# Experts' weights loaded in pairs of units: 32 KB contiguous per partition, two transfers of 64 partitions

## The chip, the cores and the metric

The kernel runs on one core of a Trainium2 chip. The metric is the device time of one execution in microseconds, the lower the better. A core has TensorE (matrix products into PSUM), VectorE, ScalarE, GpSimd and SyncE, whose queue (SPq in the profile) issues nearly all transfers here. The profile calls the engines PE (matmul) and PEld (load of the stationary operand), DVE, ACT, POOL and SP. Transfers from HBM into SBUF are carried by 16 DMA engines.

## What is computed

Two transformer blocks over 256 tokens of 1024 channels, all in float32. The first block is a hybrid mixer (HGRN2 and Mamba-2) with a gated feed-forward. The second has a modulation by a condition vector, a retention and convolution mixer, and at its end a mixture of 16 experts, which is the part that this change is about:

```
aff = softmax(h @ w_router + b_router)          # 256 tokens x 16 experts
gate, idx = top_k(aff.T, 32)                    # each expert picks 32 tokens
xs = h[idx]                                     # 16 x 32 x 1024
a = xs @ w_gate[e];  u = xs @ w_up[e]           # 1024 x 2048 each
y = (silu(a) * u) @ w_down[e] * gate            # 2048 x 1024
out = sum over experts of y, added at rows idx
```

Each expert has three float32 matrices of 8 MB, 24 MB in all, and 16 experts make 403 MB (in units of 10^6 bytes) that are read once. Each element of them is used for 32 tokens only.

## The kernel before

All weights stream through a ring of RING = 6 slots in SBUF, each a UNIT of 4096 float32 per partition, 16 KB on each of 128 partitions, 2 MB together. While the expert phase begins, five more places (`extra`, in the arena, two of them in halves called `parted` and `down_parts`) take units of the first expert. An expert is 12 units: 0 to 3 of `w_gate`, 4 to 7 of `w_up`, 8 to 11 of `w_down`. `expert_unit` issues one unit as one transfer over 128 partitions. A gate or up unit is 256 rows of the matrix, and partition p holds rows 2p and 2p+1 of it (index k), so that its 16 KB lie contiguous in HBM. A down unit is 512 rows, four rows (index j) for each partition, again 16 KB contiguous.

The order of work around this:

- SyncE's queue issues in program order. Before each unit it waits on the semaphore `units_used`, which TensorE raises after each unit that it has used. Unit n may go into its slot when unit n - 6 has been used. `BEGUN` (3) is the number of units of expert 1 that are issued ahead of the loop. The loop `Fori` issues 12 units for each turn, and after it come the last expert's units up to 10. Its unit 11 comes in three pieces (`LAST`), cut by columns, so that the tail can start early.
- TensorE's `expert(e)` waits for the selection `sel`, gathers the 32 tokens with matmuls against `xtok` (line 1359), turns the result (1365), and after DVE has scaled it (`xs`) makes the products with the eight gate and up units (1379, 16 matmul instructions for each unit). `unit_loaded` holds each unit back until its slot's semaphore says that it has landed. Then the hidden activations are turned (1390), the four down units follow (1403, again 16 for each unit), and the result is scattered into the output sums by matmuls (1410).
- `xs` needs rows of gains and shifts in the numbering of the gathered channels (`perm6`). TensorE makes them once before the first expert, at line 1330: 8 matmuls with `pick`, a strided view of the identity, for v in two sources, k in 2 and half in 2. Behind them on TensorE stand `spread_rows(gain7, 4)` (line 1173), `keep_busy(4)` (four 128-column matmuls on the identity whose result nobody reads, line 1294), and the transposes of the finished selection (1337), which wait for DVE's `router_steps` 7: DVE finds the top 32 of each expert with four rounds of MAX8 and MATCH_REPLACE8 (2517, 2518), a comparison, a scan and a product (2519 to 2522).
- Of the first expert's units, nine are in place before the expert phase; unit 11 is issued only when `units_used` shows that its first unit has been used, and all later transfers stand behind it in the SP queue.

The lines that the diff touches:

Of the kernel before, what the change touches and what calls it, by code (L numbers as in the profile page):

```python
# [23 lines left out]
P = 128  # L24
# [15 lines left out]
NE, CAP, DE = 16, 32, 2048  # L40
RING = 6
RING1 = 5
# [112 lines left out]
def build(nc, a, out):  # L155
    with ExitStack() as ctx:
# [17 lines left out]
        ring = sb("ring", [P, RING, UNIT])  # L174
# [26 lines left out]
        ps = ctx.enter_context(nc.psum_tensor("ps", [P, 8, 512], F32))  # L201
# [26 lines left out]
        ident = cs("ident")  # L228
# [23 lines left out]
        at = A.at + 5 * T  # L252
# [90 lines left out]
        xs = A.take(KT, CAP)  # L343
        ye = A.take(D)
        gx = A.take(2 * P)
        EXTRA = 5
# [46 lines left out]

        EARLY = [0, 1, 2, RING - 1]
        TURN = EARLY + [3, 4]
        FIRST = len(EARLY) + EXTRA


        def place(i, first):

            if first and len(EARLY) <= i < FIRST:
                return extra(i - len(EARLY))
            return ring[:, unit_slot(i, first), :]
# [5 lines left out]
        FIRST_SLOTS = [unit_slot(i, True) for i in range(12) if not len(EARLY) <= i < FIRST]  # L409


        def expert_rows(tokens, kt):

            return tokens.rearrange("t (b p k) -> t b k p", p=P, k=2)[:, kt // 2, kt % 2, :]

        def slot(u):
            return ring[:, u % RING1, :]

        units = []

# [34 lines left out]
        for i in range(11):  # L455
# [3 lines left out]
            w = kview(a["ffn_w_up"][0])  # L459
# [14 lines left out]
        slot_count = [0] * RING  # L474
# [73 lines left out]
        def rounded(c):  # L548

            nk = chunks[c][1].shape[1]  # L550
            at = (c % HB) * KT * P
            return ring[:, RING - 1, at:at + nk * P].rearrange("p (k c) -> p k c", k=nk)

# [19 lines left out]
        def _(sp):  # L573
# [71 lines left out]
            def expert_used(n):  # L645
                return lambda: sp.wait_ge(ev("units_used"), n)

            def expert_unit(wait_free, e, i, after=0, first=False):


                dst = None if first and i == 7 else place(i, first)
                if i < 8:
                    w = a["w_gate_2" if i < 4 else "w_up_2"][0, after:][e]
                    src = w.rearrange("(b p k) c -> b p k c", p=P, k=2)[i % 4]
                    if dst is None:
                        wait_free()
                        for k in range(2):
                            sp.dma_start(parted[k], src[:, k, :]).then_inc(ev("extra3_loaded"), 16)
                        return
                    dst = dst.rearrange("p (k c) -> p k c", k=2)  # L660
                else:
                    w = a["w_down_2"][0, after:].rearrange("e f c -> (e f) c")[bass.ds(e * DE, DE), :]
                    src = w.rearrange("(b p j) c -> b p j c", p=P, j=4)[i - 8]
                    dst = dst.rearrange("p (j c) -> p j c", j=4)
                wait_free()
                if first and len(EARLY) <= i < FIRST:
                    sp.dma_start(dst, src).then_inc(ev(f"extra{i - len(EARLY)}_loaded"), 16)
                else:
                    sp.dma_start(dst, src).then_inc(ev(f"slot{unit_slot(i, first)}_loaded"), 16)


            def down_part(n):

                src = a["w_down_2"][0, 0].rearrange("(b p j) c -> b p j c", p=P, j=4)[0]
                sp.dma_start(down_parts[n], src[:, 2 * n:2 * n + 2, :]).then_inc(ev("extra4_loaded"), 16)

            last_of = [[u for u in range(U0) if u % RING1 == s] for s in range(RING1)]
# [18 lines left out]
                    expert_unit(expert_used(UX + i - RING - EXTRA + 1), 0, i, first=True)  # L696
            for n in range(12, 12 + len(EARLY) + EXTRA + RING - 12):
                expert_unit(expert_used(UX + n - RING - EXTRA + 1), 1, n - 12)
            BEGUN = len(EARLY) + EXTRA + RING - 12
            with sp.Fori(0, NE - 2) as e:  # L700
                for i in range(BEGUN, 12 + BEGUN):

                    expert_unit(expert_used(e * 12 + (12 + UX + i - RING + 1)), e, i % 12, 1 + i // 12)
            for i in range(BEGUN, 11):
                expert_unit(expert_used((NE - 1) * 12 + (UX + i - RING + 1)), NE - 1, i)

            sp.wait_ge(ev("units_used"), (NE - 1) * 12 + (UX + 11 - RING + 1))
            rest = a["w_down_2"][0, NE - 1].rearrange("(b p j) c -> b p j c", p=P, j=4)[3]
# [11 lines left out]
        def _(pe):  # L720
# [602 lines left out]
            mm.then_inc(ev("router_products"), 1)  # L1323


            pick = ident.rearrange("p (a k) -> p k a", k=2)
            for v, src in enumerate((gain6, mod[:, 24:32, 0])):
                for k in range(2):
                    for half in range(2):
                        mm = pe.matmul(ps[64 * half:64 * half + 64, 6, 8 * v:8 * v + 8].rearrange("p (b k) -> p k b", k=2)[:, k, :],  # L1330
                                       pick[:, k, :], src.rearrange("p (b h) -> p h b", h=2)[:, half, :], start=True, stop=True)
            mm.then_inc(ev("rows_turned"), 1)
            spread_rows(gain7, 4).then_inc(ev("rows_turned"), 1)
            keep_busy(4)
# [5 lines left out]

            def unit_loaded(e, i, first):

                if first and len(EARLY) <= i < FIRST:
                    pe.wait_ge(ev(f"extra{i - len(EARLY)}_loaded"), 32 if i >= 7 else 16)
                    return
                s = unit_slot(i, first)
                if first:
                    pe.wait_ge(ev(f"slot{s}_loaded"), slot_count[s] + 16 * (1 + FIRST_SLOTS[:FIRST_SLOTS.index(s) + 1 if i < FIRST + 2 else None].count(s) - 1))  # L1350
                else:
                    pe.wait_ge(ev(f"slot{s}_loaded"), (e - 1) * 32 + (slot_count[s] + 16 * (FIRST_SLOTS.count(s) + 1 + i // RING)))

            def expert(e, first=False, last=False):

                pe.wait_ge(ev("sel_ready"), e + 1)
                for w in range(2):
                    for b in range(4):
                        mm = pe.matmul(ps[32 * b:32 * b + 32, 3, 0:256], sel[:, w, :], xtok[:, w, 256 * b:256 * b + 256], start=w == 0, stop=w == 1)
                mm.then_inc(ev("gathered"), 1)  # L1360
                if first:
                    keep_busy(1)
# [73 lines left out]
            def last_outputs():  # L1436

                for i in range(3):
                    unit_loaded(NE - 1, 8 + i, False)
                    for c in range(3):  # L1440
                        last_products(i, c)
                unit_loaded(NE - 1, 11, False)
# [1162 lines left out]
```

## Time and profile before

| | |
|---|---|
| median of 3 runs | 1627.14 us (1626.53 to 1629.29) |
| the profiled execution's own time | 1626.27 us |
| its span, first to last instruction | 1624.5 us |
| instructions | 21513 |
| PE busy / PEld busy | 1283.9 us / 774.3 us |
| moved by DMA | 524.06 MB in 94083 packets |
| SP queue's waits for TensorE's line 1379 (experts' gate and up) | 517.4 us in 121 waits |

The span is shorter than the execution's own time by 1.8 us, which lies before the first and behind the last instruction. A busy PE is an instruction in flight and not a full array. A packet in the DMA views is one contiguous piece that one DMA engine moved; the packets under 512 B in the expert phase are those that raise the semaphores, one for each engine and transfer.

### The profile page before, as it was taken

Reading aid. Unit: us, or ns where it says so; the run is one execution under the profiler, and the core shown is the slowest. Engines: PE = TensorE matmul, PEld = TensorE weight load, DVE = VectorE, ACT = ScalarE, POOL = GpSimd, SP = SyncE. Lnnn points to the kernel's source line nnn. Section 1 sums busy time; section 2 is a strip of 40 time slices with the busy share of each in tenths; the row PEclk is TensorE's granted clock in tenths of the full one; section 3 lists DMA queues with packets and bytes.
Section 4 is the critical chain, followed back from the end, with each engine's and each line's share of the span. In section 5 each row is a group of like instructions: output and inputs, shape, how many; then the busy total and the mean of one; then the engine's idle time right before and its main releaser. Section 6 shows DMA issues by size and latency. Waiting matters only on the chain.

```text
span 1624.5 us, 21513 instructions
## 1 busy us (share of the span) xinstructions
PE 1283.9 (79%) x8640; PEld 774.3 (48%) x8640; DVE 519.8 (32%) x967; ACT 505.3 (31%) x764; POOL 301.5 (19%) x231
## 2 busy tenths in 40 slices
PE   9999999999999999997656766665666665666565
PEld 8788899989999889652111111111111111111111
DVE  6775887576773735430000000000000000000001
ACT  7754777566654426521100100110110110010001
POOL 0000211779789545100000000000000000000000
PEclk9999999999999999999888768878887897887887
DMA  8855422295434723689999999999999999999997
GB/s 317 331 202 197 156 105 104 104 332 188 168 143 173 281 104 105 256 349 427 427 429 428 428 430 427 428 429 428 430 427 428 430 427 428 429 428 430 427 428 293
DMA packets 94083, 524.06 MB, mean 323 GB/s; under 512 B 8089, under 2 KB 32177, under 8 KB 66113
## 3 DMA queue, kind: packets, MB, share of 16 engines
q1 hardware_dynamic: 93681, 522.61, 79.3%
q8 instruction: 46, 0.75, 0.2%
q10 hardware_dynamic: 336, 0.54, 0.1%
q14 instruction: 20, 0.16, 0.0%
HBM read 522.08 MB, written 1.05 MB: 322 GB/s over the span
## 4 chain that ended last, share of the span: by engine, by line
DMA 48%; PE 42%; DVE 4%; ACT 3%; SPq 2%; issue 1%; DVEq 0%; ACTq 0%
DMA ring<-in_w_down 24%; DMA ring<-in_w_up 23%; PE ps L757 8%; PE ps L761 8%; PE ps L758 7%; PE ps L1379 4%; PE ps L1403 3%; PE ps L1275 2%; PE ps L997 2%; SPq L575 2%; PE ps L1048 1%; PE ps L739 1%; SPq L588 1%; PE ps L921 1%; DMA ring<-in_w_in 1%
## 5 line engine op out<-in xcount | busy, mean ns | idle before, releaser
L1379 PE MATMUL ps<-ring,arena 128*32 128x512 f32 x1984 | 289.8, 722 | 167.7 <-DMA ring<-in_w_up 120.6
L757 PE MATMUL ps<-arena_r,ring_r 128*128 128x258 f32 (+3 forms) x1144 | 341.6, 299 | 2.1 <-DVE uT_r L2268 1.1
L761 PE MATMUL ps<-arena_r,ring_r 128*128 128x258 f32 (+3 forms) x1144 | 332.9, 291 | 0.0
L1403 PE MATMUL ps<-ring,arena 128*32 128x512 f32 x944 | 162.5, 824 | 94.2 <-DMA ring<-in_w_down 88.1
L1379 PEld LDWEIGHTS ps<-ring,arena 128*32 128x32 f32 x1984 | 61.5, 121 | 364.0 <-DMA ring<-in_w_up 182.7
L758 PE MATMUL ps<-arena_r,ring_r 128*128 128x256 f32 (+3 forms) x792 | 232.3, 293 | 0.0
L757 PEld LDWEIGHTS ps<-arena_r,ring_r 128*128 128x128 f32 x1144 | 216.6, 189 | 10.1 <-issue 6.2
L1861 POOL TENSOR_TENSOR ring_r<-ring,ring_r 128x512 fp32r<-128x512 f32 (+1 forms) x113 | 153.7, 1360 | 359.8 <-PE ps L923 241.7
L761 PEld LDWEIGHTS ps<-arena_r,ring_r 128*128 128x128 f32 x1144 | 215.7, 189 | 2.9
L1864 POOL TENSOR_TENSOR arena<-arena 128x512 f32<-128x512 f32 x1 | 1.3, 1320 | 959.0 <-ACT arena L1845 959.0
L1476 ACT ACTIVATE ring_r<-ring 128x1024 fp32r<-128x1024 f32 (+1 forms) x145 | 149.8, 1040 | 43.1 <-PE ps L758 32.0
L1862 POOL TENSOR_TENSOR ring_r<-ring,ring_r 128x512 fp32r<-128x512 f32 (+1 forms) x113 | 153.9, 1362 | 0.0
L758 PEld LDWEIGHTS ps<-arena_r,ring_r 128*128 128x128 f32 x792 | 149.5, 189 | 4.4 <-issue 1.2
L1403 PEld LDWEIGHTS ps<-ring,arena 128*32 128x32 f32 x944 | 30.4, 132 | 210.8 <-DMA ring<-in_w_down 151.7
L1819 ACT ACTIVATE arena<-ps 128x512 f32<-128x512 f32 x16 | 9.6, 597 | 312.2 <-PE ps L1390 312.2
L2552 DVE TENSOR_TENSOR arena<-arena,ps 128x512 f32<-128x512 f32 x16 | 11.0, 688 | 282.9 <-PE ps L1379 282.9
L758 PE MATMUL ps<-uT_r,ring_r 128*128 128x258 f32 x352 | 99.5, 283 | 0.0
L2556 DVE COPY arena<-ps 128x512 f32<-128x512 f32 x15 | 10.4, 692 | 273.3 <-PE ps L1403 273.3
L1823 ACT ACTIVATE arena<-ps 128x512 f32<-128x512 f32 x15 | 9.0, 597 | 250.6 <-PE ps L1403 250.6
L1410 PE MATMUL ps<-arena 128*128 128x512 f32 x120 | 60.6, 651 | 13.5 <-DVE arena L2556 13.5
L758 PEld LDWEIGHTS ps<-uT_r,ring_r 128*128 128x128 f32 x352 | 66.8, 190 | 0.0
L1817 ACT ACTIVATE arena<-ps 128x512 f32<-128x512 f32 x16 | 9.6, 597 | 166.3 <-PE ps L1379 166.3
(418 smaller groups left out, 1483.3 us busy)
## 6 DMA issues: line engine op xcount, KB each, us to landing
ring<-in_w_gate SPq DMA_DIRECT2D x64, 2048.0 KB, 26.0
ring<-in_w_down SPq DMA_DIRECT2D x62, 2048.0 KB, 26.1
ring<-in_w_up SPq DMA_DIRECT2D x60, 2048.0 KB, 24.6
ring<-in_w_in SPq DMA_DIRECT2D x19, 2048.0 KB, 12.2
ring<-in_w_ada SPq DMA_DIRECT2D x12, 2048.0 KB, 11.6
ring<-in_ffn_w_up SPq DMA_DIRECT2D x22, 1024.0 KB, 7.9
ring<-in_w_out SPq DMA_DIRECT2D x6, 2048.0 KB, 8.0
ring<-in_ffn_w_down SPq DMA_DIRECT2D x4, 2048.0 KB, 7.8
```

The source lines that it names most:

```text
L575: sp.dma_start(dst, src, **kw).then_inc(ev(sem), 16)
L757: pe.matmul(o, hi[:, k, :], r_(xhi(k0 + k)), start=first and k == 0, stop=False)
L758: mm = pe.matmul(o, hi[:, k, :], r_(xlo(k0 + k)), start=False, stop=False)
L761: mm = pe.matmul(o, lo[:, k, :], r_(xhi(k0 + k)), start=False, stop=last and k == nk - 1)
L997: mm = pe.matmul(o[:, 0:T], w[:, k, :], uT[:, k, :], start=k == 0, stop=k == KT - 1)
L1275: mm = pe.matmul(ps[:, 4 + 2 * w + cb, :], x[:, w * P:w * P + P], slot(u_out2[cb]).rearrange("p (k c) -> p k c", k=KT)[:, i, :], start=n = ...
L1379: mm = pe.matmul(ps[32 * j:32 * j + 32, half, :], xs[:, kt, :], wk[:, 512 * j:512 * j + 512], start=kt == 0, stop=kt == KT - 1)
L1403: mm = pe.matmul(ps[32 * j:32 * j + 32, half, :], heT[:, j, 32 * i:32 * i + 32], wj[:, 512 * half:512 * half + 512], start=i == 0, stop=i ...
L1410: mm = pe.matmul(ps[:, 4 + b, :], Gt[:, w * P:w * P + P], ye[:, half * 512:half * 512 + 512], start=first, stop=False, skip_group_check=True)
L1476: act.activation(r_(rounded(c)), chunks[c][1], ACT.Copy).then_inc(ev("w_hi"), 1)
L1861: pool.tensor_tensor(r_(w[:, 0:mid, :]), w[:, 0:mid, :], hi[:, 0:mid, :], ALU.subtract).then_inc(ev("w_lo"), 1)
L1862: pool.tensor_tensor(r_(w[:, mid:, :]), w[:, mid:, :], hi[:, mid:, :], ALU.subtract).then_inc(ev("w_lo"), 1)
```

## The change

Six edits belong together:

1. `expert_pair` replaces `expert_unit` for experts 1 (from unit 4) to 15 (up to unit 9). A pair of units (4 MB) is laid out so that partition p holds four rows of gate or up, or eight rows of down, 32 KB contiguous in HBM and in two neighbouring slots of the ring. It is issued as two transfers, partitions 0 to 63 and 64 to 127, each raising the semaphore of one of the two slots. One wait on `units_used` stands ahead of both, for the later unit of the pair. Units outside the pairs keep one transfer of 128 partitions with 16 KB each, taken as halves (h) of the 32 KB runs.
2. `RING_AT` places the slots so that the two of a pair are neighbours.
3. `unit_loaded` waits for both slots of a pair before the first of its units is used, also for units 0 to 3 of expert 1, which are loaded singly; only the last expert's units 10 and 11 are waited for alone.
4. `BEGUN` becomes 4, so that the loop starts on an even unit.
5. The columns are renumbered: the gather reads `xtok` in runs of 2 floats at a pitch of 4, the gate and up products read the unit in runs of 4 floats at a pitch of 8 (`hidden_cols`). Sizes and counts of these matmuls stay the same.
6. The rows for `perm6` are made by 32 matmuls (4 q by 4 parts by 2 sources, each 32 output partitions and 2 columns) in place of 8 (64 partitions, 4 columns), and the `keep_busy(4)` behind `spread_rows(gain7, 4)` is gone.

```
+        RING_AT = [5, 0, 1, 3, 4, 2]
...
+        def gate_rows(w):
+            return w.rearrange("(b p h k) c -> b h p k c", p=P, h=2, k=2)
+        def down_rows(w):
+            return w.rearrange("(b p h j) c -> b h p j c", p=P, h=2, j=4)
...
+            def expert_pair(n, e, i, after=0):
+                if i < 8:
+                    w = a["w_gate_2" if i < 4 else "w_up_2"][0, after:][e]
+                    src = w.rearrange("(b p q) c -> b p (q c)", p=P, q=4)[i % 4 // 2]
+                else:
+                    w = a["w_down_2"][0, after:].rearrange("e f c -> (e f) c")[bass.ds(e * DE, DE), :]
+                    src = w.rearrange("(b p q) c -> b p (q c)", p=P, q=8)[(i - 8) // 2]
+                s0, s1 = unit_slot(i, False), unit_slot(i + 1, False)
+                assert RING_AT[s1] == RING_AT[s0] + 1
+                dst = ring[:, RING_AT[s0]:RING_AT[s0] + 2, :].rearrange("p a b -> p (a b)")
+                sp.wait_ge(ev("units_used"), n)
+                sp.dma_start(dst[0:64], src[0:64]).then_inc(ev(f"slot{s0}_loaded"), 16)
+                sp.dma_start(dst[64:128], src[64:128]).then_inc(ev(f"slot{s1}_loaded"), 16)
...
-            BEGUN = len(EARLY) + EXTRA + RING - 12
+            BEGUN = len(EARLY) + EXTRA + RING - 12 + 1
+            expert_unit(expert_used(UX + 12 + BEGUN - 1 - RING + 1), 1, BEGUN - 1)
             with sp.Fori(0, NE - 2) as e:
-                for i in range(BEGUN, 12 + BEGUN):
-                    expert_unit(expert_used(e * 12 + (12 + UX + i - RING + 1)), e, i % 12, 1 + i // 12)
-            for i in range(BEGUN, 11):
-                expert_unit(expert_used((NE - 1) * 12 + (UX + i - RING + 1)), NE - 1, i)
+                for i in range(BEGUN, 12 + BEGUN, 2):
+                    expert_pair(e * 12 + (12 + UX + i + 1 - RING + 1), e, i % 12, 1 + i // 12)
+            for i in range(BEGUN, 10, 2):
+                expert_pair((NE - 1) * 12 + (UX + i + 1 - RING + 1), NE - 1, i)
+            expert_unit(expert_used((NE - 1) * 12 + (UX + 10 - RING + 1)), NE - 1, 10)
...
-            pick = ident.rearrange("p (a k) -> p k a", k=2)
+            pick = ident.rearrange("p (a q) -> p q a", q=4)
             for v, src in enumerate((gain6, mod[:, 24:32, 0])):
-                for k in range(2):
-                    for half in range(2):
-                        mm = pe.matmul(ps[64 * half:64 * half + 64, 6, 8 * v:8 * v + 8].rearrange("p (b k) -> p k b", k=2)[:, k, :],
-                                       pick[:, k, :], src.rearrange("p (b h) -> p h b", h=2)[:, half, :], start=True, stop=True)
+                for q in range(4):
+                    for part in range(4):
+                        mm = pe.matmul(ps[32 * part:32 * part + 32, 6, 8 * v:8 * v + 8].rearrange("p (b q) -> p q b", q=4)[:, q, :],
+                                       pick[:, q, :], src.rearrange("p (b h) -> p h b", h=4)[:, part, :], start=True, stop=True)
             mm.then_inc(ev("rows_turned"), 1)
             spread_rows(gain7, 4).then_inc(ev("rows_turned"), 1)
-            keep_busy(4)
...
+                for n in [i] if alone else [i - i % 2, i - i % 2 + 1]:
+                    s = unit_slot(n, False)
+                    pe.wait_ge(ev(f"slot{s}_loaded"), (e - 1) * 32 + (slot_count[s] + 16 * (FIRST_SLOTS.count(s) + 1 + n // RING)))
...
-                        mm = pe.matmul(ps[32 * b:32 * b + 32, 3, 0:256], sel[:, w, :], xtok[:, w, 256 * b:256 * b + 256], start=w == 0, stop=w == 1)
+                        mm = pe.matmul(ps[32 * b:32 * b + 32, 3, 0:256], sel[:, w, :], gathered(w, b), start=w == 0, stop=w == 1)
...
-                                mm = pe.matmul(ps[32 * j:32 * j + 32, half, :], xs[:, kt, :], wk[:, 512 * j:512 * j + 512],
+                                mm = pe.matmul(ps[32 * j:32 * j + 32, half, :], xs[:, kt, :], hidden_cols(wk, j),
```

with the two new views

```
gathered(w, b):      xtok[:, w, :].rearrange("t (b p h k) -> t b h p k", p=P, h=2, k=2)[:, b // 2, b % 2]
hidden_cols(wk, j):  wk.rearrange("p (b q h l) -> p b h q l", q=P, h=2, l=4)[:, j // 2, j % 2]
```

## Rows read from the trace of the kernel before

**Rows 1.** The chain that ended last (start us, us, what), expert phase.

```profile
935.88 3.47 PE ps L1379 x16
939.50 25.70 DMA ring<-in_w_down
965.24 3.69 PE ps L1403 x16
969.08 25.50 DMA ring<-in_w_up
```

**Rows 2.** Windows: us, PE, PEld, DVE, ACT, POOL, PEclk, DMA share, GB/s.

```profile
710.00:715.00 5.00, 5.00 (x29) 4.85 (x29) 3.94 (x13) 1.65 (x3) 0.00 (x0) 0.63 0.99 416
715.00:720.00 5.00, 4.00 (x41) 2.20 (x43) 1.96 (x6) 2.38 (x3) 0.00 (x0) 1.00 0.12 44
725.00:730.00 5.00, 5.00 (x50) 1.50 (x46) 0.42 (x1) 0.60 (x1) 0.00 (x0) 1.00 1.02 436
800.00:1600.00 800.00, 506.17 (x3060) 125.00 (x3064) 51.49 (x123) 62.82 (x81) 0.00 (x0) 0.83 1.01 429
```

**Rows 3.** DMA view, window 800 to 1600 us, 16 KB pieces.

```profile
DMA packets 23542, 342.81 MB, mean 429 GB/s; under 512 B 2619, under 2 KB 2619, under 8 KB 2619
```

**Rows 4.** DMA view, window 533 to 543 us, 2 KB pieces of w_in.

```profile
DMA packets 1925, 3.88 MB, mean 388 GB/s; under 512 B 32, under 2 KB 32, under 8 KB 1925
```

**Rows 5.** DMA view, window 348 to 357 us, 1 KB pieces of ffn_w_up.

```profile
DMA packets 3118, 3.14 MB, mean 349 GB/s; under 512 B 48, under 2 KB 3118, under 8 KB 3118
```

**Rows 6.** Timeline ahead of the first expert (start us, us, engine, line, instruction, count).

```profile
708.55 0.60 PE L1330 MATMUL ps<-small,cst 128*64 128x4 f32 x8
...
709.51 3.78 PE L1173 MATMUL ps<-cst,small 128*128 128x128 f32 x16
...
713.08 1.33 PE L1294 MATMUL ps<-cst 128*128 128x128 f32 x8
...
713.61 0.41 DVE L2522 TENSOR_TENSOR arena<-arena 16x256 f32<-16x256 f32 x1
714.35 0.20 PEld L1337 LDWEIGHTS ps<-cst,arena 16*128 16x128 f32 x2
...
715.83 1.07 PE L1359 MATMUL ps<-arena,hT 128*32 128x256 f32 x16 [0.33 <-DVEq L2534]
...
720.93 0.33 SPq L669 DMA_DIRECT2D ring<-in_w_down  x1
```

**Rows 7.** Windows as in rows 2, one us each.

```profile
712.00:713.00 1.00, 1.00 (x7) 1.00 (x6) 0.90 (x5) 0.00 (x0) 0.00 (x0) 0.50 0.93 393
714.00:715.00 1.00, 1.00 (x9) 0.85 (x9) 0.22 (x2) 0.98 (x2) 0.00 (x0) 1.00 1.00 418
```

**Rows 8.** Timeline of PE, the turn from one expert to the next.

```profile
1019.09 1.92 PE L1403 MATMUL ps<-ring,arena 128*32 128x512 f32 x16 [1.39 <-DMA ring<-in_w_down]
1023.97 3.40 PE L1403 MATMUL ps<-ring,arena 128*32 128x512 f32 x16 [2.96 <-DMA ring<-in_w_down]
1028.26 3.67 PE L1410 MATMUL ps<-arena 128*128 128x512 f32 x8 [0.89 <-DVE arena L2556]
...
1036.27 5.36 PE L1379 MATMUL ps<-ring,arena 128*32 128x512 f32 x48 [1.12 <-DVEq L2541]
```

**Rows 9.** DMA view, window 2.1 to 3.0 us: loads of 32 and of 16 partitions.

```profile
DMA packets 132, 0.22 MB, mean 241 GB/s; under 512 B 44, under 2 KB 84, under 8 KB 132
...
q1 hardware_dynamic: 100, 0.21, 86.7%
q10 hardware_dynamic: 32, 0.01, 4.0%
```

**Rows 10.** DMA view, window 4.4 to 5.4 us: loads of 112 partitions.

```profile
DMA packets 103, 0.37 MB, mean 369 GB/s; under 512 B 13, under 2 KB 13, under 8 KB 103
...
q1 hardware_dynamic: 103, 0.37, 101.8%
```

More of the change, by code:

```diff
@@ L402, in place @@
                 return extra(i - len(EARLY))
-            return ring[:, unit_slot(i, first), :]
+            return ring[:, RING_AT[unit_slot(i, first)], :]
         def unit_slot(i, first):
@@ L409, in build @@
         FIRST_SLOTS = [unit_slot(i, True) for i in range(12) if not len(EARLY) <= i < FIRST]
-        def expert_rows(tokens, kt):
-            return tokens.rearrange("t (b p k) -> t b k p", p=P, k=2)[:, kt // 2, kt % 2, :]
+        def gate_rows(w):
+            return w.rearrange("(b p h k) c -> b h p k c", p=P, h=2, k=2)
+        def down_rows(w):
+            return w.rearrange("(b p h j) c -> b h p j c", p=P, h=2, j=4)
         def slot(u):
-            return ring[:, u % RING1, :]
+            return ring[:, RING_AT[u % RING1], :]
         units = []
@@ L551, in rounded @@
             at = (c % HB) * KT * P
-            return ring[:, RING - 1, at:at + nk * P].rearrange("p (k c) -> p k c", k=nk)
+            return ring[:, RING_AT[RING - 1], at:at + nk * P].rearrange("p (k c) -> p k c", k=nk)
         seq = []
@@ L653, in expert_unit @@
                     w = a["w_gate_2" if i < 4 else "w_up_2"][0, after:][e]
-                    src = w.rearrange("(b p k) c -> b p k c", p=P, k=2)[i % 4]
+                    src = gate_rows(w)[i % 4 // 2, i % 2]
                     if dst is None:
@@ L662, in expert_unit @@
                     w = a["w_down_2"][0, after:].rearrange("e f c -> (e f) c")[bass.ds(e * DE, DE), :]
-                    src = w.rearrange("(b p j) c -> b p j c", p=P, j=4)[i - 8]
+                    src = down_rows(w)[(i - 8) // 2, i % 2]
                     dst = dst.rearrange("p (j c) -> p j c", j=4)
@@ L669, in expert_unit @@
                     sp.dma_start(dst, src).then_inc(ev(f"slot{unit_slot(i, first)}_loaded"), 16)
+            def expert_pair(n, e, i, after=0):
[11 more added lines that the diff above has]
+                sp.dma_start(dst[64:128], src[64:128]).then_inc(ev(f"slot{s1}_loaded"), 16)
             def down_part(n):
-                src = a["w_down_2"][0, 0].rearrange("(b p j) c -> b p j c", p=P, j=4)[0]
+                src = down_rows(a["w_down_2"][0, 0])[0, 0]
                 sp.dma_start(down_parts[n], src[:, 2 * n:2 * n + 2, :]).then_inc(ev("extra4_loaded"), 16)
@@ L698, in _ @@
                 expert_unit(expert_used(UX + n - RING - EXTRA + 1), 1, n - 12)
-            BEGUN = len(EARLY) + EXTRA + RING - 12
+            BEGUN = len(EARLY) + EXTRA + RING - 12 + 1
+            expert_unit(expert_used(UX + 12 + BEGUN - 1 - RING + 1), 1, BEGUN - 1)
             with sp.Fori(0, NE - 2) as e:
-                for i in range(BEGUN, 12 + BEGUN):
-                    expert_unit(expert_used(e * 12 + (12 + UX + i - RING + 1)), e, i % 12, 1 + i // 12)
-            for i in range(BEGUN, 11):
-                expert_unit(expert_used((NE - 1) * 12 + (UX + i - RING + 1)), NE - 1, i)
+                for i in range(BEGUN, 12 + BEGUN, 2):
[3 more added lines that the diff above has]
+            expert_unit(expert_used((NE - 1) * 12 + (UX + 10 - RING + 1)), NE - 1, 10)
             sp.wait_ge(ev("units_used"), (NE - 1) * 12 + (UX + 11 - RING + 1))
-            rest = a["w_down_2"][0, NE - 1].rearrange("(b p j) c -> b p j c", p=P, j=4)[3]
+            rest = down_rows(a["w_down_2"][0, NE - 1])[1, 1]
             for c, (c0, c1) in enumerate(LAST):
@@ L1339, in _, with unit_loaded @@
             keep_busy(3)
-            def unit_loaded(e, i, first):
+            def unit_loaded(e, i, first, alone=False):
                 if first and len(EARLY) <= i < FIRST:
@@ L1350, in unit_loaded, with gathered, hidden_cols @@
                     pe.wait_ge(ev(f"slot{s}_loaded"), slot_count[s] + 16 * (1 + FIRST_SLOTS[:FIRST_SLOTS.index(s) + 1 if i < FIRST + 2 else None].count(s) - 1))
-                else:
-                    pe.wait_ge(ev(f"slot{s}_loaded"), (e - 1) * 32 + (slot_count[s] + 16 * (FIRST_SLOTS.count(s) + 1 + i // RING)))
+                    return
+                for n in [i] if alone else [i - i % 2, i - i % 2 + 1]:
+                    s = unit_slot(n, False)
+                    pe.wait_ge(ev(f"slot{s}_loaded"), (e - 1) * 32 + (slot_count[s] + 16 * (FIRST_SLOTS.count(s) + 1 + n // RING)))
+            def gathered(w, b):
+                return xtok[:, w, :].rearrange("t (b p h k) -> t b h p k", p=P, h=2, k=2)[:, b // 2, b % 2]
+            def hidden_cols(wk, j):
+                return wk.rearrange("p (b q h l) -> p b h q l", q=P, h=2, l=4)[:, j // 2, j % 2]
             def expert(e, first=False, last=False):
@@ L1438, in last_outputs @@
                 for i in range(3):
-                    unit_loaded(NE - 1, 8 + i, False)
+                    unit_loaded(NE - 1, 8 + i, False, alone=i == 2)
                     for c in range(3):
                         last_products(i, c)
-                unit_loaded(NE - 1, 11, False)
+                unit_loaded(NE - 1, 11, False, alone=True)
                 last_products(3, 0).then_inc(ev("last_pe"), 1)
```

## Prediction

> **What bounds the kernel now.** I read the chain of waits first. Behind 764 us it is made of DMA stretches of some 25 us, each followed by 2 to 4 us of TensorE on the unit that has just landed [rows 1]: the end of the kernel is set by the stream of expert weights. The windows show the same from the transfers' side: between 800 and 1600 us the 16 DMA engines are busy all the time and carry 429 GB/s, while TensorE holds an instruction for 506 of the 800 us [rows 2]. So in this stage the price of a transfer counts in full and TensorE's time counts for nothing until it exceeds the transfers'. The third thing to see is a hole: between 715 and 720 us the DMA share is 0.12 [rows 2]. The queue has run dry there, because the next transfer waits for the first expert's first used unit, and SP issues it at 720.93 us [rows 6]. From there on the stream runs without a break to the end, so whatever moves that 720.93 moves the end by as much. The edits therefore come down to two numbers: the length of one transfer, and the start of the stream.
>
> **The length of a transfer.** Three clean stretches give the price of a packet, each a saturated stream of one piece size. Taking the semaphore packets off:
> 16 KB pieces: 23542 - 2619 = 20923 in 800 us on 16 engines, 12,800,000 / 20923 = 611.8 ns for each, and 8 on each engine make a 2 MB transfer: 4894 ns [rows 3].
> 2 KB pieces: 1925 - 32 = 1893 in 10 us, 84.5 ns each, 64 to a 2 MB transfer and engine: 5409 ns [rows 4].
> 1 KB pieces: 3118 - 48 = 3070 in 9 us, 46.9 ns each, 128 for 2 MB: 6004 ns [rows 5].
> For the same bytes, 56 packets more cost 515 ns (9.2 ns each) and 120 more cost 1110 ns (9.25 ns each). Two steps with the same slope are a good reason to treat the price as bytes plus 9.2 ns a packet. The bytes of 2 MB then take 4894 - 8 x 9.2 = 4820 ns, which is 435 GB/s.
> In pairs each engine moves the same 128 KB in 4 packets of 32 KB, 37 ns less: 4857 ns in place of 4894, 0.75% off. No row shows a piece over 16 KB, so the bounds are: nothing gained, if a 32 KB run is still carried as two packets; and twice the term, 74 ns, as if all the packet price went. I take 37 ns, since the line is straight over a factor of 16 in size.
> Transfers that become pairs: 14 turns of the loop with 12, and 6 of the last expert, 174 in all. 174 x 37 ns = 6.4 us gained (0 to 12.9).
> The Trainium skill, "DMA: Bandwidth & Descriptors", section "Why small descriptors are slow (HBM only)", puts a fixed overhead of about 3 cycles on each packet beside 32-byte beats. By it the packets' share would be about 3.5 ns each at 850 MHz and the gain an estimated 2.5 us; the rows show 9.2 ns and decide.
>
> **The start of the stream.** The 8 pick matmuls are 16 instruction pairs on TensorE in 0.96 us (708.55 to 709.51), 60 ns a pair [rows 6]. 32 matmuls are 64 pairs, 3.84 us, so the following spread_rows (3.78 us) ends at 713.29 + 2.88 = 716.17 instead of 713.29. Before, `keep_busy(4)` filled TensorE until 714.4, and DVE's last step of the selection ended at 714.02, after which the transposes of L1337 started at 714.35 [rows 6]. So before, DVE set the time and TensorE's 1.3 us of idle-filling hid; without them TensorE is still the later one, and L1337 starts at about 716.2, 1.85 us late. What is late next: DVE's copy of the selection, the gather, `xs`, the first unit of expert 0, SP's issue at 720.93, and with it every later transfer. ScalarE's steps beside it (bc from the spread rows, then the table load ahead of the eviction of the gathered rows) move by the 2.9 us and end just within the new start of that eviction.
> Bounds: with 32 columns in place of 64 for the stationary operand a pair might cost 40 ns, which gives 64 x 40 = 2.56 us and a delay of 0.6 us. The other end is the clock. TensorE's granted clock is 0.50 (1.2 GHz) at 712 us and 1.00 (2.4 GHz) at 714 us, having risen after more than 3 us of dense L1173 [rows 7]. If the rise came only after the gather and the first unit, those (1.07 us and 1.8 us [rows 6, 8]) would take twice as long, and the delay would be 1.85 + 2.9 = 4.8 us. I take 1.85, as the same spread_rows still stand between.
>
> **Edits at no cost, and what hides them.** One wait for a pair: a pair is freed when both its units are used, so two transfers enter the queue late by one unit's products, 1.9 us (3.4 to 3.5 at the low clock). Three pairs of slots exist. At the turn of an expert, the last down unit lands at 1023.97 and gate unit 0 starts at 1036.27 [rows 8]. With pairs both last down units are used behind the landing, 2 x 3.5 us, then 8.9 us of scatter, gather and `xs`, then 2 x 3.5 us for the next pair: its slots are free 22.9 us after the landing. The queue then holds two pairs (19.6 us) plus the one that was issued 7 us behind the landing, 29.4 us of work. The slack is 6.5 us, enough for the 1 to 2 us from issue to first packet; if it were gone, each microsecond missing would cost one for each expert, 15 us over the kernel. `unit_loaded` waiting for both units costs nothing inside the stream for the same reason, and at the end the units 10 and 11 are waited for alone, so the tail stays. The placement of slots, BEGUN, and one single transfer moved ahead of the loop change no sum.
> The strided operands (runs of 8 and of 16 bytes) stand on TensorE: no row shows such a moving operand. From below their cost is nothing. From above, a unit of 3.5 us at the low clock could double to 7 us, over the 4.9 of its transfer; but a TensorE that is busy is granted the full clock, at which the unit takes 1.8 to 1.9 us [rows 8], and doubled it still fits under 4.9. It decides only from a factor of about 2.5. I take nothing.
>
> **Sum.** -6.4 + 1.85 = -4.5 us. The profiled execution took 1626.27 us (span 1624.5 and 1.8 around it), 0.9 below the median of 1627.14, and the change is set against the median: 1622.6 us, -0.28%.
>
> **The rivals.**
> *The packet price does not shrink.* A 32 KB run goes as two packets, or the 9.2 ns belong to the amount and the slope was chance. Against it: two slopes agree. For it: nothing above 16 KB was seen. Then only the late start is left: 1627.1 + 1.85 = 1629.0 us (1627.7 to 1632 by the bounds), no measurable change unless the clock adds its part.
> *Half the partitions, slower packets (the other side).* A transfer now writes 64 partitions and all 16 engines work on the same half. Place: each of the 174 transfers. The trace's only loads on few partitions are at the start. Between 2.1 and 3.0 us the engines are 90.7% busy, 13.1 engine-us, with 48 packets of 4 KB onto 32 and 16 partitions; 84 small ones at some 9 to 28 ns take about 2 of it, which leaves 11.1 / 48 = 230 ns a packet, where the line gives 9.2 + 151 = 160 ns: 1.44 times [rows 9]. With 112 partitions it is 16.3 / 90 = 181 ns at most, 1.13 times [rows 10]. Those stretches are short, and full of starts and ends, which also lengthen packets, and 64 partitions lie between. If 1.44 held, each transfer would take 7.0 us, 174 x 2.15 = 375 us more: about 2000 us. The mechanism decides from tiny amounts on: 37 ns in a transfer (0.75%) eat the gain, 56 ns make the kernel measurably slower. Against the full price: consecutive transfers go to opposite halves, and engines that have drifted apart by one transfer would write both halves at once.
> The Trainium skill speaks against this change: "SBUF — State Buffer", section "Door 1: The DMA port swizzle", says that partitions 0 to 63 reach only 8 of the 16 write ports, gives 196 GB/s for 64 partitions against 328 for 128 at 1 MB, and finds that two transfers to opposite halves gain only 6%. By its ports each paired transfer would take twice 4.89 us and the kernel an estimated 1627 + 851 = 2478 us; rows 9 point the same way without reaching the factor.
> *The queue runs dry or the strided operands bind.* By the slack above this needs 6.5 us more at each turn, or a factor of 2.5. It would show at each expert; at 2 us each it gives +30 - 4.5, about 1653 us.
>
> **How the numbers follow.** Forecast (packets shrink, late start) 0.53; packet price unchanged 0.25; half the partitions 0.18; dry queue or strided operands 0.04. The prediction is 1622.6 us. The forecast's own range is 1616 (12.9 gained, 1.85 lost) to 1626 (4.8 us late); with the second case it reaches to 1631. That leaves out the last two, 0.22, of which small amounts of slower packets still lie inside. A measurement of this kernel tells about 0.2% (3.3 us) from no change. Faster by more: most of the forecast, less the part where the start costs more than 3 us, 0.53 - 0.02 = 0.51. Within: the second case and that part, less a little for 1631, 0.27. Slower: the last two cases, 0.22.
>
> **What would show it.** In the profile after: between 800 and 1600 us about 10,500 packets of 32 KB and some 432 GB/s (right), or 21,000 packets and 429 (packets as before), or a rate well below 429 with the DMA share still full (half partitions). The chain's DMA pieces stay, and TensorE's L1330 group has 64 instructions over about 3.8 us, with L1337 at 716 us. SP's issue behind the hole comes at 722.8 us in place of 720.93. A DMA share under 1.00 at the turns of experts would mean a dry queue; L1379 over 722 ns in the mean by much, strided operands. Wrong would be above all a rate of the paired transfers off 432 GB/s to either side.

## The result, and the profile after

The changed kernel takes 2515.8 us (2515.34 to 2517.06, 4 runs) against 1627.1 us, a ratio of 1.546 with a 95% interval of 1.544 to 1.548. It is 889 us slower. The forecast was 1622.6 us in a range of 1616 to 1631; of the rivals it is the one that half the partitions make slower packets, to which the prediction gave 0.18 and a time of about 2000 us.

First the page of the changed kernel: its packets, and the start of the chain that ended last. "Another core or an unknown queue" is how the page names the waits for the second transfer of a pair, whose semaphore it apparently could not put down to an issue; there is only one core here, and the same page lists the idle time ahead of these products (line 1410) under `DMA ring<-in_w_up`.

```profile
DMA packets 82947, 524.06 MB, mean 208 GB/s; under 512 B 8089, under 2 KB 32177, under 8 KB 66113
...
PE 48%; another core or an unknown queue 41%; DVE 4%; DMA 4%; ACT 2%; issue 1%; DVEq 0%; SPq 0%; ACTq 0%
```

The bytes are the same to the last digit shown, and there are 11,136 packets fewer. That is 174 transfers x 16 engines x 4 packets: the 32 KB runs do go as one packet each. Then the windows of the changed kernel, in the columns of [rows 2]:

```profile
715.00:720.00 5.00, 4.01 (x41) 2.21 (x44) 1.96 (x6) 2.43 (x3) 0.00 (x0) 1.00 0.07 30
725.00:730.00 5.00, 5.00 (x50) 1.53 (x46) 0.42 (x1) 0.60 (x1) 0.00 (x0) 1.00 1.00 429
800.00:1600.00 800.00, 274.72 (x1500) 76.49 (x1500) 25.65 (x62) 32.59 (x41) 0.00 (x0) 0.66 1.00 210
```

Up to 730 us little has changed (the DMA share in the hole is 0.07 after 0.12), and the single transfers that stand ahead of the pairs still move at 429 GB/s. From the pairs on, the DMA share is 1.00 at 210 GB/s: the engines are never without work, they do it at half the pace. The DMA view of the same 800 us, beside [rows 3]:

```profile
DMA packets 6400, 167.76 MB, mean 210 GB/s; under 512 B 1280, under 2 KB 1280, under 8 KB 1280
```

6400 - 1280 = 5120 packets of 32 KB on 16 engines in 800 us is 2500 ns for each, where the line through [rows 3 to 5] gives 1214 ns. The factor is 2.06. All 16 engines take part: 80 transfers were issued in this window, and 1280 semaphore packets are 16 for each. The chain of waits has the period that follows, beside [rows 1]:

```profile
1017.33 13.34 another core or an unknown queue
...
1030.81 5.10 PE ps L1410 x32
...
1037.42 13.25 another core or an unknown queue
...
1050.81 5.30 PE ps L1434 x32
```

A pair starts on TensorE every 20.0 us (1030.81, 1050.81), and before, two units took 9.8 us. 174 transfers x (10.0 - 4.89) us = 889 us, which is the whole difference.

Last, the timeline ahead of the first expert, beside [rows 6]:

```profile
708.80 0.66 PE L1352 MATMUL ps<-small,cst 128*32 128x2 f32 x32
...
709.30 0.64 PE L1352 MATMUL ps<-mod,cst 128*32 128x2 f32 x32
...
709.87 3.47 PE L1195 MATMUL ps<-cst,small 128*128 128x128 f32 x16
...
713.85 0.41 DVE L2553 TENSOR_TENSOR arena<-arena 16x256 f32<-16x256 f32 x1
714.37 0.19 PEld L1358 LDWEIGHTS ps<-cst,arena 16*128 16x128 f32 x2 [1.23 <-DVEq L2554]
...
719.00 7.07 PE L1410 MATMUL ps<-ring,arena 128*32 128x512 f32 x64 [0.58 <-DVEq L2572]
```

The 64 instruction pairs took 1.07 us (708.80 to 709.87), 17 ns each and not 60, and the granted clock was 0.50 there in both kernels. spread_rows ended at 713.3, and TensorE then stood 1.0 us waiting for DVE (its weight load 1.23 us). The transposes start at 714.37, 0.02 later than before, and SP's issue behind the hole comes at 720.99 (720.93 before). The products of four units with the strided operand take 7.07 us at the full clock, 110 ns an instruction. Before, the same 64 instructions of the first expert also took 7.07 us, and the 48 of [rows 8] took 5.36 us, 112 ns each. The gather, whose operand now comes in runs of 8 bytes, takes 1.11 us in place of 1.07 [rows 6], which this stage does not feel. The strided operands cost next to nothing.

### The profile page after: what moved, and what is told of

Read it like the earlier page. It is cut to its first block, busy times and chain, and to the rows that moved or that the text cites. A ratio compares the mean times of both kernels' runs of the same rounds, so it can differ in the third digit from the quotient of the medians.

```text
span 2514.2 us, 21685 instructions
## 1 busy us (share of the span) xinstructions
PE 1339.8 (53%) x8680; PEld 806.3 (32%) x8680; DVE 519.8 (21%) x967; ACT 505.3 (20%) x764; POOL 301.5 (12%) x231
## 4 chain that ended last, share of the span: by engine, by line
PE 48%; another core or an unknown queue 41%; DVE 4%; DMA 4%; ACT 2%; issue 1%; DVEq 0%; SPq 0%; ACTq 0%
PE ps L1410 14%; PE ps L1434 7%; PE ps L779 5%; PE ps L783 5%; PE ps L780 5%; DMA ring<-in_w_down 4%; PE ps L1441 2%; PE ps L1019 1%; PE ps L1297 1%; PE ps L1390 1%; PE ps L1070 1%; PE ps L761 1%; PE ps L943 0%; PE ps L846 0%
## 5 line engine op out<-in xcount | busy, mean ns | idle before, releaser
L1410 PE MATMUL ps<-ring,arena 128*32 128x512 f32 x1984 | 350.1, 871 | 708.1 <-DMA ring<-in_w_up 417.4
L1410 PEld LDWEIGHTS ps<-ring,arena 128*32 128x32 f32 x1984 | 85.7, 153 | 949.8 <-issue 864.3
L1434 PE MATMUL ps<-ring,arena 128*32 128x512 f32 x944 | 166.6, 871 | 376.9 <-DMA ring<-in_w_down 376.9
L1434 PEld LDWEIGHTS ps<-ring,arena 128*32 128x32 f32 x944 | 42.0, 153 | 490.9 <-issue 490.9
L2579 DVE COPY arena<-ps 128x256 f32<-128x256 f32 x16 | 6.8, 425 | 447.7 <-PE ps L1417 447.7
```

The costliest lines, as they stand in the source:

```text
L1434: mm = pe.matmul(ps[32 * j:32 * j + 32, half, :], heT[:, j, 32 * i:32 * i + 32], wj[:, 512 * half:512 * half + 512], start=i == 0, stop=i ...
```

## The experiments

All are edits of the changed kernel at the two lines that issue a pair, unless said otherwise. Times with an interval are of 5 to 11 runs; the others are one run each, which is enough where the cases lie 900 us apart. Where they lie 5 to 70 us from the changed kernel, the measure is that kernel's own spread of 1.7 us over 4 runs.

**Partitions and run lengths apart.** Three runs fill the square of 64 or 128 partitions by 16 or 32 KB.

```
p128_32k
+                sp.dma_start(dst, src).then_inc(ev(f"slot{s0}_loaded"), 16)
+                sp.nop().then_inc(ev(f"slot{s1}_loaded"), 16)
p128_16k
+                sp.dma_start(dst[:, 0:UNIT], src[:, 0:UNIT]).then_inc(ev(f"slot{s0}_loaded"), 16)
+                sp.dma_start(dst[:, UNIT:2 * UNIT], src[:, UNIT:2 * UNIT]).then_inc(ev(f"slot{s1}_loaded"), 16)
p64_16k (the halves stay; each partition gets two runs 2 MB apart, so the rows are not where the products expect them)
+                    src = w.rearrange("(b u p q) c -> b p u (q c)", u=2, p=P, q=2)[i % 4 // 2]
...
+                    src = w.rearrange("(b u p q) c -> b p u (q c)", u=2, p=P, q=4)[(i - 8) // 2]
...
+                dst = ring[:, RING_AT[s0]:RING_AT[s0] + 2, :]
```

> Each pair as one transfer of 128 partitions with 32 KB runs (4 MB); everything else as in the changed kernel. Theory A (the halves of 64 partitions are what costs): the rate comes back, and with half the packets of the kernel before a 2 MB share takes 4857 ns in place of 4894, 432 GB/s; 1627.1 - 6.4 = about 1621 us. Theory B (runs of 32 KB, or reading HBM at that pitch, are slow whatever the partitions): stays near 210 GB/s and 2500 us. Theory C (the strided operands or the waits for pairs hold the stream up): between the two, with a DMA share under 1 behind 760 us.

> Each pair as two transfers of 128 partitions, each one slot of the pair, 16 KB at every second 16 KB of HBM. Theory A: back to the packets of the kernel before, 611.8 ns each, 429 GB/s, about 1627 us, so the distance to the run with 32 KB and 128 partitions is the packet term, 6.4 us by the line and nothing if the packet price does not exist. Theory B: also fast, since no packet is over 16 KB. Theory C: slow, as pair waits and strided operands are still there.

> Two transfers of 64 partitions for a pair, but each partition gets two runs of 16 KB that lie 2 MB apart in HBM (rows land in other places than the products assume, so the experts' output is not the reference's). Theory A: as slow as the changed kernel, 2500 us, with packets of 16 KB of about 1250 ns. Theory B: fast, about 1627 us.

| | 16 KB runs | 32 KB runs |
|---|---|---|
| 128 partitions in a transfer | 1629.3 us, ratio 1.0012 (1.0003 to 1.0021) | 1622.4 us, ratio 0.9971 (0.9960 to 0.9981) |
| 64 neighbouring partitions | 2514.3 us | 2515.8 us |

The DMA view of p128_32k between 800 and 1600 us, then that of p64_16k:

```profile
DMA packets 11927, 345.16 MB, mean 431 GB/s; under 512 B 1320, under 2 KB 1320, under 8 KB 1332
```

```profile
DMA packets 11546, 168.17 MB, mean 210 GB/s; under 512 B 1282, under 2 KB 1282, under 8 KB 1282
```

The loss sits in the row and the packet term in the column. With 128 partitions, 345.16 MB in 800 us make 32,768 x 16 / 431.45 = 1215 ns for a 32 KB packet; the line had said 1214. The distance between the two runs of the upper row is 6.9 us, where the prediction's term is 6.4. Not all of the 6.9 is packets: in the profile with 16 KB runs the stream also starts later (SP's issue at 722.43 us against 721.77) and the first turn is emptier (DMA share 0.65 against 0.89 from 755 to 760 us). From the two steady rates alone, 428.6 and 431.45 GB/s, a transfer is 33 ns shorter (37 predicted), 5.7 us over the kernel. With 64 partitions a 16 KB packet takes 12,800,000 / 10,264 = 1247 ns, half of the 2500 for 32 KB: the same bytes at the same halved rate, so Theory B (long runs are slow) falls. Theory C falls with p128_32k, which keeps the pair waits and the strided operands.

**Which partitions, or how many.**

```
p64_even_odd
+                sp.dma_start(dst[0:128:2], src[0:128:2]).then_inc(ev(f"slot{s0}_loaded"), 16)
+                sp.dma_start(dst[1:128:2], src[1:128:2]).then_inc(ev(f"slot{s1}_loaded"), 16)
p32_32k_b and p32_stride4 (the PE side waits for a third semaphore too, not shown; each run has one of the last two lines)
+                third = f"extra{(4, 1, 5).index(s0)}_loaded"
+                for q, sem in enumerate((third, third, f"slot{s0}_loaded", f"slot{s1}_loaded")):
+                    sp.dma_start(dst[32 * q:32 * q + 32], src[32 * q:32 * q + 32]).then_inc(ev(sem), 16)   # p32_32k_b
+                    sp.dma_start(dst[q:128:4], src[q:128:4]).then_inc(ev(sem), 16)                         # p32_stride4
```

> As the changed kernel, two transfers of 64 partitions with 32 KB runs, but the even partitions in the first and the odd ones in the second. Theory A1 (it is the number of partitions in one transfer that counts): 2500 us. Theory A2 (it is which partitions: neighbouring halves share write paths, a transfer over the whole range reaches all of them): up to 432 GB/s and 1621 us, or a rate between if engines that work in step still meet on one path. Theory B: 2500 us.

> Each pair as four transfers of 32 neighbouring partitions with 32 KB runs. Theory P (partitions 0 to 31 are written through the same paths as 0 to 63): no slower than in halves, 2516 us. Theory S (the rate goes with the number of partitions): a quarter of the full rate, 19.6 us for each 2 MB in place of 4.9, 174 x 14.7 = 2558 us more than at full rate, about 4180 us.

> Each pair as four transfers of 32 partitions with 32 KB runs, every fourth partition, against the run with 32 neighbouring ones, which took 2518 us. If it is only which partitions a transfer writes and not how many: 432 GB/s and about 1623 us. If 32 partitions are too few for 16 engines, whatever their places: 2500 us.

Even and odd partitions: 1623.2 us. Quarters of 32 neighbouring ones: 2518.4 us. Quarters of every fourth one: 1623.9 us. Their windows from 800 to 1600 us, in this order:

```profile
800.00:1600.00 800.00, 510.77 (x3080) 152.70 (x3082) 52.02 (x125) 64.00 (x83) 0.00 (x0) 0.81 1.00 432
```

```profile
800.00:1600.00 800.00, 273.66 (x1502) 74.84 (x1501) 25.62 (x62) 33.19 (x42) 0.00 (x0) 0.66 1.01 210
```

```profile
800.00:1600.00 800.00, 514.13 (x3080) 149.00 (x3084) 51.99 (x125) 64.35 (x83) 0.00 (x0) 0.81 1.00 432
```

So it is not the number of partitions in a transfer (32 spread ones run at 432 GB/s, 32 neighbouring ones at the same 210 as 64), and not the size or number of the transfers (four of 1 MB for a pair are as good as two of 2 MB). It is which partitions one transfer writes. The reads are not what differs: a unit transfer of the kernel before reads one contiguous 2 MB of HBM, as each half does, and moved at 429 GB/s, while p64_16k reads two separate pieces of 1 MB and stayed at 210.

The Trainium skill, "SBUF — State Buffer", section "Door 1: The DMA port swizzle", says that partitions 0 to 31 and 0 to 63 both reach the same 8 of 16 ports. By its formula the partitions 0, 4, 8 and so on reach all 16. It gives an asymptote of about 218 GB/s for 8 ports; the traces show 210. The traces have no view of single ports, so the runs show which sets of partitions are slow and the ports are the skill's reason for it.

**Both halves in flight, and engines out of step.** The two halves of a pair are issued within a microsecond. Why do they not fill all paths together?

```
p64_two_queues: SP issues only dst[0:64]; in ScalarE's expert loop, at the same counts:
+                act.wait_ge(ev("units_used"), e * 12 + (UX + to))
+                act.dma_start(dst[64:128], src[64:128]).then_inc(ev(f"slot{s1}_loaded"), 16)
...
p64_alt16k_b: four transfers, lower, upper, lower, upper
...
+                    rows, cols = slice(64 * (q % 2), 64 * (q % 2) + 64), slice(UNIT * (q // 2), UNIT * (q // 2) + UNIT)
+                    sp.dma_start(dst[rows, cols], src[rows, cols]).then_inc(ev(sem), 16)
p64_offset_b: once, ahead of the first pair
+            sp.dma_start(arena[0:8, extra_at:extra_at + 2 * UNIT], spare[0:8]).then_inc(ev("extra0_loaded"), 16)
```

> As the changed kernel, but only the lower half of each pair is issued by SP; the upper half is issued from ScalarE's queue, in the expert loop, at the same counts of used units. Theory T (the 16 engines carry both queues, but each works its two rings side by side, so that packets for the lower and for the upper half are in flight together and use all write paths): near 432 GB/s, about 1630 us. Theory U (the queues alternate packet by packet and all engines still write one half at a time): 210 GB/s and about 2515 us. The Trainium skill, SBUF - State Buffer, section 'Can I just issue two DMAs to hit both halves?', says 6% more than one half alone: about 223 GB/s and an estimated 2460 us.

> Each pair as four transfers of 64 partitions with 16 KB runs: lower half, upper half, lower half, upper half. An engine now changes halves after 64 KB and not after 128 KB, as in the run with even and odd partitions, where 64 partitions were fast. Theory P with a coarse step: all engines change at the same time, so still 210 GB/s and 2515 us. Theory R (the engines work ahead over some packets, and a change of the path after 64 KB is often enough): near 429 GB/s and 1630 us.

> As the changed kernel (halves 0 to 63 and 64 to 127, 32 KB runs), with one more load ahead of the first pair, once: 8 partitions of 32 KB into memory that nobody reads. A DMA over 8 partitions can be spread over 8 of the 16 engines at most, so it sets these behind the others. Theory P (engines meet on shared write paths only because all of them write the same half at the same time, in step): if the load sets half of the engines back by about one transfer, the two groups write different halves from then on and nothing brings them into step again; the rate returns to about 432 GB/s and the kernel to some 1625 us; set back by a part d of a transfer they give 2 - d of the time. Theory Q (a transfer as such is limited to half the rate by the half that it writes, or the engines fall back into step): 210 GB/s and 2516 us as before, plus some 5 us once.

Measured: 2447.7, 2481.7 and 2510.8 us. The window 800 to 1600 us of the run with two queues:

```profile
800.00:1600.00 800.00, 283.64 (x1548) 72.70 (x1540) 26.33 (x63) 15.22 (x28) 0.00 (x0) 0.66 1.00 219
```

Both queues had transfers for opposite halves pending (each carried half of the bytes, their transfers landed in the median 42 to 51 us after the issue, and the DMA share was 1.00), and the rate rose from 210 to 219 GB/s only, by 4%. The Trainium skill, "SBUF — State Buffer", section "Can I just issue two DMAs to hit both halves?", says 6% over one half alone (the prediction gives this figure under the section on the ports). With it a transfer would take 10.0 / 1.06 = 9.43 us and the kernel an estimated 2417 us; the 2460 us of the expectation above is a slip. 2447.7 were measured. Changing halves after 64 KB in place of 128 KB gives 214 GB/s.

The load on 8 partitions took 5 us off, in a single run. It was meant to set half of the engines back by about one transfer, and it was too small for that, as the page of the run shows beside that of the changed kernel:

```profile
DMA packets 82963, 524.32 MB, mean 209 GB/s; under 512 B 8097, under 2 KB 32185, under 8 KB 66121
```

It added 16 packets, 8 of them semaphores: 8 engines got one 32 KB packet each, and a transfer has four. So d in Theory P is 1/4 by packets, and the theory would give 1.75 of the full-speed time, about 1622 + 174 x 0.75 x 4.86 = 2256 us. 2510.8 us speak against the version in which a set-back lasts. The profile does not show single DMA engines, so whether they fall back into step, or step has nothing to do with it, is not shown. What stays open is why pending transfers for the other half do not fill the idle paths.

**Only the down pairs in halves.**

```
+                if i % 12 < 8:
+                    sp.dma_start(dst, src).then_inc(ev(f"slot{s0}_loaded"), 16)
+                    sp.nop().then_inc(ev(f"slot{s1}_loaded"), 16)
+                    return
```

> Gate and up pairs as one transfer of 128 partitions, only the 29 down pairs (58 transfers) in halves of 64. If the cost lies in each halved transfer alone, 58 of 174 bear it: 1622 + 58 x (10.0 - 4.86) = 1920 us. If full transfers between them let the engines drift apart so that halves no longer meet, well under that; if halved transfers also slow their neighbours, above.

2011.4 us, 91 more than the sum said. So whole transfers between them do not bring the halves back to speed. The window 800 to 1600 us:

```profile
800.00:1600.00 800.00, 366.32 (x2140) 102.12 (x2140) 36.53 (x88) 46.42 (x59) 0.00 (x0) 0.71 0.97 303
```

The DMA share is 0.97: here the engines are idle at times, probably because two slow pairs keep four of the six slots for 40 us. The gathers of experts 1 and 15 start at 749.40 and 1929.73 us, so an expert takes 84.3 us on average, against 4 x 10.0 + 8 x 4.86 = 78.9; over these 14 that is 76 of the 91 us. The 3% of idle make 2.5 of the 5.4 us. The rest was not followed up, so it stays open whether a halved transfer also slows its neighbours.

**The start and the first turn of the fast version.** In two more runs the `keep_busy(4)` was put back into p128_32k, and in the second the pairs also start only at unit 10 of expert 1.

```
p128_32k_busy_b and p128_late
             spread_rows(gain7, 4).then_inc(ev("rows_turned"), 1)
+            keep_busy(4)
p128_late
-            BEGUN = len(EARLY) + EXTRA + RING - 12 + 1
-            expert_unit(expert_used(UX + 12 + BEGUN - 1 - RING + 1), 1, BEGUN - 1)
+            BEGUN = 10
+            for i in range(len(EARLY) + EXTRA + RING - 12, BEGUN):
+                expert_unit(expert_used(UX + 12 + i - RING + 1), 1, i)
```

> The run with one transfer of 128 partitions and 32 KB for a pair, with the keep_busy(4) that the change took away put back behind spread_rows. In that run TensorE's granted clock was 0.66 between 715 and 720 us and SP's issue behind the hole came at 721.77 us, against 1.00 and 720.93 before. Theory K (the missing idle-filling costs the clock and with it the start of the stream): the issue comes back to about 721.0 and the time falls by 0.8 us or somewhat more, to about 1621.5. Theory L (the start varies from run to run whatever stands there): 1622.4 as without.

> The run with one 4 MB transfer for a pair and keep_busy(4) put back, with the pairs starting only at unit 10 of expert 1; units 3 to 9 of expert 1 are loaded singly, each as soon as its slot is free. Between 752 and 762 us the DMA queue of the run without this ran dry (DMA share 0.13 at 756 to 758), because only one pair had been issued between 739 and 758 us. Theory: some 2 us of the hole close, less 6 units that have 4 packets more on each engine (0.2 us): about 1620 us. Rival: the hole only moves to the next turn, 1621.8 us.

With keep_busy: 1621.8 us, ratio 0.9968 (0.9956 to 0.9980), which can't be told from 0.9971 without it. SP's issue came at 720.88 us in place of 721.77; first the window of p128_32k, then that of p128_32k_busy_b:

```profile
715.00:720.00 5.00, 4.50 (x33) 2.77 (x35) 1.44 (x5) 2.33 (x3) 0.00 (x0) 0.66 0.06 23
715.00:720.00 5.00, 4.00 (x40) 2.12 (x43) 1.96 (x6) 2.42 (x3) 0.00 (x0) 1.00 0.07 26
```

Over all 14 profiles the issue comes between 720.88 and 723.66 us, and two things move it. One is the start of the transposes, 714.01 to 715.81. The other is the way from there to the issue: 6.6 us in the five profiles in which the granted clock is 0.99 or 1.00 between 715 and 720 us, and 7.4 to 8.0 us in the nine in which it is 0.50 to 0.76. All three profiles with keep_busy (before, p128_32k_busy_b, p128_late) are among the five, and only two of the eleven without it (the changed kernel and p64_two_queues). So the traces lean to Theory K, that the idle-filling keeps this stretch at the high clock and saves 0.8 us or more, while the times are too close together to show it.

p128_late takes 1620.8 us, ratio 0.9962 (0.9948 to 0.9975). Its median is the lowest of all, but its interval overlaps that of 1621.8. What the trace shows is that its hole is closed. First p128_32k_busy_b, then p128_late:

```profile
755.00:760.00 5.00, 5.00 (x40) 1.32 (x36) 0.00 (x0) 0.00 (x0) 0.00 (x0) 0.76 0.65 220
```

```profile
755.00:760.00 5.00, 5.00 (x44) 1.29 (x40) 0.00 (x0) 0.00 (x0) 0.00 (x0) 0.89 0.99 406
```

The DMA share is 0.65 from 755 to 760 us, and 0.99 in p128_late; the rate behind 800 us is 431 GB/s, that of p128_32k. The profiled span is 1.7 us shorter (1618.7 and 1620.4) although its stream began 1.2 us later.

## Why the prediction was wrong, point by point

- **What bounds the kernel:** right. The stream of expert weights sets the end in both kernels, and 889 us of the 889 lie in the paired transfers.
- **Number of packets:** right. 4 packets of 32 KB for each engine and transfer.
- **The length of a transfer, 4857 ns: this step failed.** It measured 10,000 ns. The term was read off three stretches of transfers over 128 partitions and applied to transfers over 64 neighbouring ones. Taken for what those rows cover it holds: with 128 partitions 1215 ns a packet and 5.7 us by the steady rates (6.9 between the times), predicted 1214 and 6.4.
- **The rival that came true** was priced too low and given too little. The price of 1.44 came from loads of 32 and 16 partitions that lasted 0.9 us [rows 9], mixed with starts and ends; a stream that lasts shows 2.06. The prediction's estimate from the ports of the Trainium skill ("SBUF — State Buffer", section "Door 1: The DMA port swizzle") was 2478 us, 38 us off.
- **The argument against its full price failed:** that consecutive transfers go to opposite halves and engines that drift apart would write both. A deep queue of alternating halves stayed at 210 GB/s for 1750 us, two queues at once gave 219, and neither a change of halves every 64 KB nor one extra load brought more than 35 us.
- **The start, +1.85 us:** too large, and for a wrong reason. 17 ns a pair and not 60; the transposes still waited for DVE, and in the changed kernel's profile the issue moved by 0.06 us. The 60 ns had been taken from matmuls with 64 stationary columns, and the lower bound of 40 ns was also too high. In most profiles without keep_busy the clock did make the start late (in p128_32k a granted clock of 0.66 and an issue 0.84 us late), which the prediction had only as its other bound.
- **Pair waits at no cost:** right in the steady stream (DMA share 1.00), not at the first turn. There only one pair is issued between 739 and 758 us, and in the fast version the queue runs dry for 0.5 us (DMA share 0.89 from 755 to 760 us in p128_32k) to 1.8 us (0.65 in p128_32k_busy_b). The slack of 6.5 us had been worked out for a full queue, which the first turn does not have.
- **Strided operands at no cost:** right, 7.07 us for 64 instructions in both kernels.
- **The range:** its upper end of 1631 us is 1627.1 + 4.8, which is 1631.9, the 1632 of the rival's own text. Nothing hangs on it.

With the partitions left whole, the forecast of 1622.6 us meets the 1622.4 of p128_32k. That it meets it to 0.2 us is partly luck: the start was 0.84 us late in place of 1.85, the packets gave 5.7 us in place of 6.4, and the first turn cost something that the sum had at nothing.

## What to carry to other kernels

If a load of this kind has to be cut, cut it along the free dimension or in strided partitions, and not into blocks of 32 or 64 neighbouring ones: the block runs at half the rate, and a second block in flight doesn't make up for it. Fewer and longer packets are worth their 9 ns each, which is little but can be forecast. And before a fitted line is applied, list what all its points have in common (here 128 partitions): a change that leaves this common ground makes the line silent, and then a rule that names the new ground weighs more than a plausible argument that it will not bite.

## What the runs showed of the hardware

- A stream of transfers over 64 or 32 neighbouring partitions moves 210 GB/s on 16 busy engines; over every second or every fourth partition 432 GB/s.
- The two halves from two queues at once: 219 GB/s. Alternating in 1 MB transfers in one queue: 214 GB/s.
- Over 128 partitions a packet costs its bytes plus 9.2 ns from 1 KB up to 32 KB (1215 ns for 32 KB, 1214 by the line).
- A load over 8 partitions of 32 KB went as 8 packets with 8 semaphore packets.
- 64 instruction pairs with 32 stationary and 2 moving columns took 1.07 us at a granted clock of 0.50, 17 ns each.
- A moving operand in runs of 16 bytes at a pitch of 32 bytes is as fast as a contiguous one (7.07 us for 64 instructions of 512 columns at the full clock, in both kernels).
